# A two-block transformer kernel: the first four projection units in the wide form, and the depthwise convolution's stationaries built by GpSimd

## The reference

```python
def conformer_conv(a, gate, dw_kernel, dw_bias, ln_g, ln_b):
    u = a * jax.nn.sigmoid(gate)
    pad = CONV_WIDTH // 2                      # CONV_WIDTH = 31
    y = lax.conv_general_dilated(u, dw_kernel[:, None, :], window_strides=(1,), padding=[(pad, pad)],
        dimension_numbers=("NWC", "WIO", "NWC"), feature_group_count=u.shape[-1])
    return jax.nn.silu(layer_norm(y + dw_bias, ln_g, ln_b))
...
h = rms_norm(x, norm1_g)
a, gate, q, k, v = jnp.split(h @ w_in, splits, axis=-1)     # 512 columns each
conv_out = conformer_conv(a, gate, ...)
attn_out = neighbourhood_attention(rms_norm(q), rms_norm(k), v, rpb)
x = x + concatenate([conv_out, attn_out]) @ w_out
h = rms_norm(x, norm2_g)
x = x + (silu(h @ w_gate) * (h @ w_up)) @ w_down
```

## Time and profile before

| | |
|---|---|
| median of 3 runs | 1037.72 us (1037.16 to 1037.75) |
| profiled execution | 1037.5 us, of which the span from first to last instruction is 1035.7 us |
| PE busy | 1022.3 us, 99% of the span |
| DVE / ACT / POOL busy | 735.2 / 552.5 / 82.9 us |
| granted TensorE clock | 0.999 of full |
| longest waits of PE before its matmuls | 1.5 (first constants), 1.5 (parameters), 1.3 (big<-skew), 0.7 (DVE, first half of wlo), 0.6 (ACT kT), 0.6 (DVE wlo) |

### The profile page before, as it was taken

The page is one execution under the profiler, slowest core; times in us unless marked ns, Lnnn a source line. Parts: engine busy times, 40 slices in busy tenths (PEclk is TensorE's granted clock), DMA queues, the critical chain, the costliest instruction groups (busy, mean ns, idle before and its releaser), DMA issues.

```text
span 1035.7 us, 15604 instructions
## 1 busy us (share of the span) xinstructions
PE 1022.3 (99%) x5757; PEld 870.9 (84%) x5757; DVE 735.2 (71%) x1104; ACT 552.5 (53%) x722; POOL 82.9 (8%) x82
## 2 busy tenths in 40 slices
PE   8999999999999999999999999999999999999997
PEld 7876788888888888898888888888888988888886
DVE  6986777666667699867766566667998777655654
ACT  6556574545447545664644444475366646444444
POOL 1000000000001219000000000011280000000000
PEclk9999999999999999999999999999999999999999
DMA  9994356554466553267465653675632765565521
GB/s 320 232 258 136 122 163 200 204 205 162 147 212 210 172 167 119 88 221 260 138 229 172 215 182 126 210 214 168 189 102 82 246 222 188 181 215 188 174 89 41
DMA packets 130974, 185.69 MB, mean 179 GB/s; under 512 B 4169, under 2 KB 106207, under 8 KB 130911
## 3 DMA queue, kind: packets, MB, share of 16 engines
q1 hardware_dynamic: 130823, 184.84, 55.2%
q10 hardware_dynamic: 88, 0.04, 0.0%
HBM read 183.23 MB, written 2.15 MB: 179 GB/s over the span
## 4 chain that ended last, share of the span: by engine, by line
PE 93%; DMA 2%; ACT 2%; DVE 1%; issue 1%; SPq 1%; ACTq 0%; DVEq 0%
PE wide L588 29%; PE wide L595 15%; PE acc L551 9%; PE acc L552 9%; PE acc L553 9%; PE wide L571 3%; PE wide L564 3%; PE wide L565 3%; PE wide L551 2%; PE wide L552 2%; PE wide L553 2%; DMA big<-skew 1%; PE acc L731 1%; PE acc L765 1%; PE acc L752 1%
## 5 line engine op out<-in xcount | busy, mean ns | idle before, releaser
L1340 DVE TENSOR_TENSOR wlo<-raw,whi 128x2048 fp32r<-128x2048 f32 (+1 forms) x178 | 388.8, 2190 | 132.8 <-ACT whi L1010 131.4
L1010 ACT ACTIVATE whi<-raw 128x2048 fp32r<-128x2048 f32 (+1 forms) x178 | 322.1, 1819 | 61.1 <-PE acc L553 33.3
L588 PE MATMUL wide<-uhl,whi 128*128 128x512 f32 x1312 | 315.8, 392 | 0.0
L588 PEld LDWEIGHTS wide<-uhl,whi 128*128 128x128 f32 x1312 | 242.7, 188 | 51.5 <-issue 1.7
L595 PEld LDWEIGHTS wide<-uhl,wlo 128*128 128x128 f32 x1312 | 168.2, 191 | 6.4
L595 PE MATMUL wide<-uhl,wlo 128*128 128x256 f32 x1312 | 170.2, 283 | 0.0
L551 PE MATMUL acc<-whi,mhi 128*128 128x512 f32 x376 | 147.8, 393 | 0.6 <-DVE wlo L1340 0.6
L552 PE MATMUL acc<-wlo,mhi 128*128 128x512 f32 x376 | 146.8, 390 | 0.0
L553 PE MATMUL acc<-whi,mlo 128*128 128x512 f32 x376 | 146.4, 389 | 0.0
L553 PEld LDWEIGHTS acc<-whi,mlo 128*128 128x128 f32 x376 | 70.6, 188 | 15.1
L551 PEld LDWEIGHTS acc<-whi,mhi 128*128 128x128 f32 x376 | 70.8, 188 | 14.7 <-DVE wlo L1340 1.0
(11 more groups left out here) (261 smaller groups left out, 1205.2 us busy)
## 6 DMA issues: line engine op xcount, KB each, us to landing
raw<-in_w_in SPq DMA_DIRECT2D x49, 1024.0 KB, 5.3
raw<-in_w_mlp_up SPq DMA_DIRECT2D x32, 1024.0 KB, 5.5
raw<-in_w_mlp_down SPq DMA_DIRECT2D x32, 1024.0 KB, 4.9
raw<-in_w_gate SPq DMA_DIRECT2D x11, 1024.0 KB, 5.4
raw<-in_w_up SPq DMA_DIRECT2D x11, 1024.0 KB, 5.4
raw<-in_w_down SPq DMA_DIRECT2D x11, 1024.0 KB, 5.4
raw<-in_w_mix_out SPq DMA_DIRECT2D x8, 1024.0 KB, 5.4
raw<-in_w_out SPq DMA_DIRECT2D x4, 1024.0 KB, 10.7
```

What stands on the lines that cost most here:

```text
L588: pe.matmul(col[2 * n + c][:], whi_v(u)[:, f, c * P:c * P + P], uhl[:, f, :], start=f == 0, stop=False)
L1010: act.activation(whi[:, u.buf, 0:size], raw[:, u.slot, 0:size], ACT.Copy).then_inc(w_hi, 1)
L1340: dve.tensor_tensor(wlo[:, u.buf, 0:size], raw[:, u.slot, 0:size], whi[:, u.buf, 0:size].bitcast(F32), ALU.subtract).then_inc(w_lo, 1)
```

## The change

The first four units go through the wide form; unit j uses the pair of banks `wide[j % 2]`. For each, ACT copies the upper half into `vtok` (`low_part`) and DVE adds the lower (`halves_sum`), and PE waits for that (`a_sum`) before it uses the pair again. The transposes of x go chunk by chunk, both token halves in one bank, so that ACT and DVE make `uhi` and `ulo` in 8 pieces of 128x256. The first unit's `whi` products no longer wait for its `wlo`. The four tensor_tensor and four memsets of `tap_stationaries` go to POOL; the mask copies stay on DVE (`tap_mask`). On PE `convolve(0)` and `convolve(1)` go behind unit 7 and the turning of q. On ACT the copy of kT goes ahead of the split of unit 11. On DVE `gated` goes ahead of `scale_gate_a`.

```diff
+        def first_bank(f):
+            return (acc + [col[2], col[3]] + acc)[f][:, 0:T]
...
-            def col_features_after(k, u, bank, ready=None):
+            def first_features(u):
                 for h in range(2):
-                    if ready:
-                        ready(h)
+                    pe.wait_ge((half_hi, w_hi)[h], 1)
                     for c in range(COLS // P):
                         for f in range(4 * h, 4 * h + 4):
                             if c == 0:
-                                pe.wait_ge(u_lo, feature_count(k, f))
...
+                                pe.wait_ge(u_lo, 2 * f + 2)
+                            wide_high(u, 0, c, f)
+                    pe.wait_ge((half_lo, w_lo)[h], 1)
+                    for c in range(COLS // P):
+                        for f in range(4 * h, 4 * h + 4):
+                            mm = pe.matmul(col[c][:, 0:T], wlo_v(u)[:, f, c * P:c * P + P], uhl[:, f, 0:T],
+                                           start=False, stop=f == KD - 1)
...
-            for i in range(4):
-                turn_quarter(0, i)
...
+            for f in range(KD):
+                if f % 4 == 0:
+                    pe.wait_ge(x_in[f // 4], 16)
+                if f >= 6:
+                    pe.wait_ge(u_lo, 2 * (f - 6) + 2)
+                for t in range(NT):
+                    tr = pe.transpose(first_bank(f)[:, t * P:t * P + P], x[:, t, f * P:f * P + P], ident[:])
+                tr.then_inc(u_ps, 1)
...
             for j in range(A_OUT):
                 u = a_unit(j)
-                if 0 < j < 4:
-                    pe.wait_ge(w_lo, u.upto())
-                if j in (4, 6):
-                    pe.wait_ge(fevac, j - 2)
+                if 2 <= j <= 4:
+                    pe.wait_ge(a_sum, j - 1)
+                if j == 6:
+                    pe.wait_ge(a_sum, 4)
...
-                    col_features_after(0, u, col[0], first_half)
+                    first_features(u)
                 elif j < 4:
-                    col_features(u, col[j % 4], uhi, ulo)
+                    wide_features(u, j % 2)
...
-                if j == 6:
-                    pe.wait_ge(kst_ok, 1)
-                    pe.wait_ge(shift_in, 16 * 2 * SHIFTS)
-                    convolve(0)
-                    convolve(1)
...
+                if j == 7:
+                    pe.wait_ge(kst_ok, 1)
+                    pe.wait_ge(shift_in, 16 * 2 * SHIFTS)
+                    convolve(0)
+                    convolve(1)
...
+            def low_part(j):
+                act.wait_ge(used, a_unit(j).upto())
+                if j >= 2:
+                    act.wait_ge(glu, 1)
+                act.activation(vtok[:, j % 2, :].rearrange("p (c t) -> p c t", c=2), wide[j % 2][:, :, T:2 * T], ACT.Copy)\
+                    .then_inc(a_low, 1)
...
             split(a_unit(1))
+            low_part(0)
             split(a_unit(2))
...
+                if j == 1:
+                    low_part(1)
                 if j:
+                    if j == 9:
+                        copy_turned(0, 1, kT, gcol[:, G_KG:G_KG + 1])
                     split(a_unit(j + 2))
+                if j in (2, 3):
+                    low_part(j)
...
+            def halves_sum(j):
+                v = vtok[:, j % 2, :].rearrange("p (c t) -> p c t", c=2)
+                dve.wait_ge(a_low, j + 1)
+                dve.tensor_tensor(v, wide[j % 2][:, :, 0:T], v, ALU.add).then_inc(a_sum, 1)
...
+                if j in (2, 4):
+                    gated(j // 2 - 1)
+                if j in (2, 3):
+                    halves_sum(j)
...
-                    tap_stationaries(0)
+                    tap_mask()
...
-                if j == 8:
-                    tap_stationaries(1)
...
+            tap_stationaries(0)
+            pool.wait_ge(conv_ps, 2)
+            tap_stationaries(1)
```

More of the change, by code:

```diff
@@ L249, in build @@
         x_in = [sem(f"x_in{h}") for h in range(2)]
+        a_low = sem("a_low")
+        a_sum = sem("a_sum")
         half_in = sem("half_in")
@@ L298, in build @@
         conv_dve = sem("conv_dve")
+        mask32_ok = sem("mask32_ok")
         kst_ok = sem("kst_ok")
@@ L657, in turn_quarter @@
                 t, h = QUARTERS[i]
[L658 to L661, removed]
+                pe.wait_ge(x_new, quarter_count(k, i))
                 for c in range(4):
@@ L818, in _ @@
                 if j == 1:
[L819 to L824 removed]
+                    spread_rn(acc[3], 1)
                 if j == 7 or j == 8:
@@ L1094, in _ @@
             parameters()
-            raw_hi(0, gcol, G_N1, lambda: split_half(0))
-            split_half(1)
+            for f in range(KD):
+                act.wait_ge(u_ps, f + 1)
+                act.activation(uhi[:, f, :], first_bank(f), ACT.Copy, scale=gcol[:, G_N1 + f:G_N1 + f + 1]).then_inc(u_hi, 2)
+                if f % 4 == 3:
+                    split_half(f // 4)
             split(a_unit(1))
+            low_part(0)
             split(a_unit(2))
@@ L1461, in gated, with tap_mask @@
                 dve.wait_ge(glu, i + 1)
[L1463 to L1482 removed]
+            def tap_mask():
+                dve.wait_ge(kx_sb, 1)
+                dve.wait_ge(consts, 4)
+                for s in range(SHIFTS):
+                    at = slice(SHIFT_CH * s, SHIFT_CH * s + SHIFT_CH)
+                    ins = dve.tensor_copy(mask32[at, :], ident[at, at])
+                ins.then_inc(mask32_ok, 1)
             def conv_evac(c):
@@ L1507, in _ @@
             dve.wait_ge(par_sb, 2)
-            raw_norm(0, gcol, G_N1, None, False, lambda: split_half(0))
-            split_half(1)
+            for f in range(KD):
+                dve.wait_ge(u_hi, 2 * f + 2)
+                dve.scalar_tensor_tensor(ulo[:, f, :], first_bank(f), gcol[:, G_N1 + f:G_N1 + f + 1], uhi[:, f, :].bitcast(F32),
+                                         ALU.mult, ALU.subtract).then_inc(u_lo, 2)
+                if f % 4 == 3:
+                    split_half(f // 4)
             split(a_unit(1))
+            halves_sum(0)
             split(a_unit(2))
@@ L1842, in _, with tap_stationaries @@
             pool.tensor_copy(ident16[:], ident[:]).then_inc(wmask_ok, 1)
+            def tap_stationaries(half):
+                if half == 0:
+                    pool.wait_ge(wmask_ok, 5)
+                    pool.wait_ge(kx_sb, 1)
+                    pool.wait_ge(mask32_ok, 1)
+                kxv = kx[:].rearrange("p (g r) -> p g r", r=GROUPS)
+                for n, out in enumerate(kst):
+                    r = HALF_GROUPS * half + 2 * n
+                    g = 0 if half else DVE_SETS
+                    shape = [P, TAP_SETS - g, 2, SHIFT_CH]
+                    ins = pool.tensor_tensor(out[:, g:TAP_SETS, :, :], kxv[:, g:TAP_SETS, r:r + 2].unsqueeze(3).broadcast_to(shape),
+                                            mask32.unsqueeze(1).unsqueeze(1).broadcast_to(shape), ALU.mult)
+                link(ins)
+                for n, out in enumerate(kst):
+                    ins = pool.memset(out[SHIFT_CH * (SHIFTS - 1):P, TAP_SETS - 1, :, :], 0.0)
+                ins.then_inc(kst_ok, 1)
+            tap_stationaries(0)
+            pool.wait_ge(conv_ps, 2)
+            tap_stationaries(1)
             pool.wait_ge(rope_in, 16)
```

55 lines of the change are left out of this document (12 added, 43 removed).

## The result

| | before | after |
|---|---|---|
| median of 8 runs, us | 1037.74 | 1040.78 |
| lowest to highest, us | 1036.17 to 1040.06 | 1040.36 to 1041.91 |
| profiled execution, us (its span) | 1037.5 (1035.7) | 1040.4 (1038.5) |
| ratio after / before | | 1.0031 [1.0018, 1.0043] |

The changed kernel is slower by 3 us. The prediction said 1037.3 with a range to 1039.1. The time lies outside the range, and the case in which contention makes it slower had been given a chance of 0.10.

What follows compares the result with a forecast made beforehand. PE bounds the kernel, with DVE the second bound of the head. A gain of 1.3 us less 0.9 of contention gave -0.4, profiled 1037.5 to 1037.1, median 1037.3; range 1035.9 to 1039.1 us.

Steps and rivals of the forecast that it cites:

- The bound and the place: PE is full from 120 us on, so whatever the head gains or loses by then stays to the end.
- before unit 4: Sign in the head: PE stands about 1.2 us before unit 4, released by DVE's sum.
- before the turning of k: Sign in the head: PE stands over 1 us before the turning of k, released by DVE.
- From the turning to the scores: Turning of k to first scores: kT's copy ahead of a split cuts 3.47 us to 2.75, gaining 0.7.
- rival 4: First four units: the wide form wins nothing on PE, every unit bound by its split; 1037.7 to 1038.5 us, chance 0.05.
- the part of the sum without contention: Gain at the first scores: 0.6 us at the turning of k and 0.7 behind it, 1.3 us in all.
- The clock step: Unit 0: PE's pace doubles 2.7 us after its products begin, ending the unit at 16.6; at 13.8, 17.1.
- rival 1: Head: the gain arrives whole, POOL leaves DVE alone and the pace doubles early; 1035.7 to 1036.4 us, chance 0.15.
- the price of contention: DVE's critical work beside POOL's turns: slowed by 0 to 0.41 in 2.29 us, 0 to 1.7 us; 0.9 taken.
- the split of 403.87: DVE's split beside busy POOL, 2.28 us, taken as a sign that POOL leaves DVE alone.
- Rival 2: DVE's critical work beside POOL: two-input operations stretch by 80% over 7 us, 5.6 us; sum +4.3, 1042 us, chance 0.10.
- all that PE wins: PE's gains between 36 and 69 us, the 1.26 at 54.19 included, end in its wait for DVE before turning k.

Runs made afterwards that it cites:

- POOL alone: The kernel before, with both turns of stationaries on POOL and nothing else of the change: 1038.04 us, ratio 0.9990.
- the turn held back: The changed kernel, with POOL's second turn of stationaries held until the scaling of k is done: 1036.25 us, ratio 0.9973.
- half-sized products: The changed kernel, with POOL's four 128x512 products of the second turn made eight of 128x256: 1038.57 us, ratio 0.9998.
- the clock kept up: The changed kernel, with 18 matmuls on zeros in PE's wait ahead of the turning of k: 1039.03 us, ratio 1.0002.

## Why the prediction was wrong

**What held.** The bound and the place were right: PE's wait for DVE near 119 us ends at 119.28 against 116.79, so that 2.5 of the 2.8 us between the spans were lost by then. PE waited before unit 4, released by DVE's sum (1.9 us against 1.2), not before the convolution, and over 1 us before the turning of k, released by DVE. POOL's turns were done at 32.5 and 67.6, before they were wanted. From the turning to the scores it was 2.87 us in the kernel with the second turn on DVE, 2.75 forecast, 3.47 before; no run moves the kT copy alone, and the kernel with POOL alone has 2.87 without that move. A wide unit took 27.23 - 21.58 = 5.65 us, as forecast, so rival 4 (nothing won on PE) is out. The change without POOL put the first scores at 71.39 instead of 73.20, where the part of the sum without contention said 1.3 less; at the second convolution (79.66 against 80.69) 1.0 was left, since the maxima took 0.7 back.

**Better than forecast.** Unit 0 started at 9.19 instead of 9.6 and ended at 15.1 instead of 16.6. The clock step was wrong: I had the pace double 2.7 us after the first product or at 13.8, and it was double almost at once. Unit 4 started at 34.8 instead of 35.6, and the gating at 31.46 instead of 32.9. That is the early doubling of rival 1; what it won was lost again in the wait for k.

**The step that failed** is the price of contention: "At 0 to 0.41 in 2.29 us that is 0 to 1.7 us; I take the middle, 0.9". It took a delay as a share of the duration. The runs show a delay per instruction, up to one whole instruction of the other engine whatever one's own length. Of a long subtraction 0.41 is 18%; a tap of 0.40 us beside products of 1.24 lost 0.80, which is 200%. The term measured 3.2 us on four taps and 0.4 on the gating, 3.6 in place of 0.9. The rows of before had it already: the split of 2.70 lost 0.41, the multiply of 1.25 lost 0.56, and no delay there was longer than POOL's own 1.04. The durations of the victims differ by a factor of three, and the delays much less. The prediction took the split of 403.87, with its 2.28 us, as a sign that POOL leaves DVE alone. POOL's timeline of the kernel before shows who paid there, and beside the subtraction of 397.22 (2.62 us):

```profile
396.25 0.74 POOL L1861 TENSOR_TENSOR y<-y,rtmp 128x256 f32<-128x256 f32 x1
...
397.77 2.67 POOL L1861 TENSOR_TENSOR y<-y,rtmp 128x256 f32<-128x256 f32 x1
...
403.88 2.74 POOL L1859 TENSOR_TENSOR rtmp<-cu,lg 128x256 f32<-128x256 f32 x1
```

Both took 2.7 us where such an instruction takes 0.6 to 0.75. The plainest row stands a little further on, in DVE's timeline:

```profile
413.62 1.69 DVE L1403 TENSOR_SCALAR nmx<-mx 128x2 f32<-128x2 f32 x1
```

This tiny instruction takes 0.17 us elsewhere. Here it ended at 415.31, 0.03 us behind a product of POOL's of 128x1024 (411.03 + 4.25 = 415.28). With a loss of up to 1.29 us for each of four taps, 5.2 us in all, the sum would have been 1037.7 - 1.3 + 5.2 = 1041.6. Rival 2 stood at 1042, but by a stretch of 80% over 7 us, which is a share of the duration as well; that its figure lies near the measured one is luck. (A slip beside it: the lower end of rival 1, 1035.7, is 2.0 us under 1037.7 and so not past the 2.1 us that the prediction calls 0.2%.)

The rule was to be had too. The Trainium skill, "SBUF — State Buffer", section "Who interferes with whom", says that whichever of the two engines issues first holds the shared pair of ports for its whole instruction and that the other one blocks, and that a DVE instruction with two inputs in SBUF meets a GpSimd instruction that reads SBUF. The trace agrees in kind (taps 1.20 instead of 0.40 us apart beside products of 1.24), and in that the maxima, with one input in PSUM, kept their 0.41 us. I had cited only the sentence that contention exists, not the one that says how it is priced.

**The consequence that was missing.** The prediction let "all that PE wins" end in the wait for k and never asked what a long wait does to PE. At 4.31 us the granted clock fell to 0.50, and that cost 1.5 us more.

**The sum as it is.** Against the version without POOL, on the traces: the turning of k 71.35 - 68.52 = 2.83 us later, the clock 4.37 - 2.87 = 1.5, less 0.7 for the maxima that PE then need not wait for. That is 3.6, and the spans differ by 1038.5 - 1034.9 = 3.6. The 2.83 is less than the 3.6 lost on DVE because the profiled execution of the changed kernel had the earlier start: its mask copies begin at 26.66, those of the version without POOL at 27.43. Counted from there the turning of k comes 3.60 us later, and the whole is 4.4 us, near the 4.2 between the medians (1040.78 and 1036.55). Against the kernel before, the change without POOL is 0.8 us shorter in the span (1.9 in the medians), and 0.8 - 3.6 is the 2.8 us by which the changed one is longer.

## What to carry to other kernels

Work on GpSimd left alone the DVE instructions that took one of their two inputs from PSUM (the maxima, 0.41 us). Where DVE reads both from SBUF, count for each DVE instruction the rest of one GpSimd instruction, not a percentage. Look at small TENSOR_SCALAR instructions in the same way: with a single tensor read one was held for 1.5 us, the row of 413.62 above. Keep rows of short DVE instructions out of such stretches, or cut the GpSimd instructions small. Where a chain gets later, look also at what the longer wait does to TensorE's clock; and before work is moved to another engine, look for work ahead of the critical wait that is needed only later.

## What the runs showed of the hardware that I had not expected

**The delay is not quite a whole instruction.** In the row of taps the pair tap and product takes 1.20 us, with products of 1.05 alone (in the kernel with the turn held back) and taps 0.40 apart: 0.25 us of the two overlap. With products of half the size (0.62 alone) the pair takes 0.77, and again 0.25 overlap.

**What waits cost the clock.** Behind waits of 1.09 us (second turn on DVE) and 1.30 (POOL alone) the way from turning to scores was 2.87 us, with the granted clock at 1.00. Waits of 2.58 (half-sized products) and 4.31 us brought 4.44 and 4.37. In the half-sized case the clock was still 1.00 when PE began again at 69.72, and fell behind that:

```profile
69.00:70.00 1.00, 0.28 (x3) 0.29 (x4) 1.00 (x2) 0.27 (x1) 0.00 (x0) 1.00 1.15 213
70.00:71.00 1.00, 1.00 (x9) 1.00 (x8) 1.00 (x1) 0.59 (x2) 0.00 (x0) 0.81 1.09 208
71.00:72.00 1.00, 1.00 (x4) 0.71 (x3) 0.86 (x1) 1.00 (x3) 0.00 (x0) 0.50 0.99 191
```

So 1.5 us were lost after the shorter wait as after the longer one.

**The start.** In the kernel before, 256 columns took 0.21 us at 12.8, the pace of 1.2 GHz, after PE had stood 0.75 us. (The granted clock of the window from 12 to 13 us reads 1.00 all the same; the starts are what I go by.) In the changed one PE went from the transposes into the products without a wait, and they ran at full pace from about 9.5:

```profile
9.19 0.72 PE L595 MATMUL wide<-uhl,whi 128*128 128x512 f32 x1
...
9.19 0.95 PE L595 MATMUL wide<-uhl,whi 128*128 128x512 f32 x2
```

The second matmul of 512 columns ends 0.23 us behind the first. Unit 0's products took 5.9 us instead of the forecast 7.0, which is 1.1 of the 1.5 us by which its end was early; the other 0.4 is its start. The wait alone does not decide it. In the kernel with the clock kept up, whose head is that of the changed kernel up to this place, PE stood 1.15 us before 9.66, and the first eight products took 2.11 us, which is full pace. There the transposes too had run at full pace, eight in 1.04 us against 1.91 in the changed kernel, although the two programs do the same until then. So the pace at the start differs from execution to execution; what sets it stays open.
